# Experts' rows without a token are skipped in the gather and in the store, which becomes an indirect transfer

## The reference, cut to what matters

```python
expert = g_idx * EXPERTS_PER_GROUP + e_idx            # 2 of 32 experts for each of T = 512 tokens
order, counts = argsort(flat_e), bincount(flat_e)     # 1024 (token, expert) pairs
x_rows = hf[row_tok]                                   # rows of each expert's block
y = (silu(xb @ w_e_gate[e]) * (xb @ w_e_up[e])) @ w_e_down[e]      # 1024->512, 1024->512, 512->1024
y = segment_sum(y_rows * row_w, row_tok)               # back to the tokens
out = rmsnorm(x + y)
```

## Time and profile before

| | |
|---|---|
| median of 3 runs | 2750.77 us |
| the profiled execution's own time | 2743.79 us |
| its span, first to last instruction | 2742.1 us |
| mean granted TensorE clock | 0.979 of full speed |
| experts, first store of a result to last | 2192.81 to 2710.28 us |
| busy over the whole span | PE 94%, DVE 72%, ACT 46%, POOL 37% |
| instructions | 38302 |

### The profile page before, as it was taken

One profiled execution on the slowest core, in us unless ns is written; L12 is line 12 of the kernel. 1 busy time (PEld: TensorE's weight loads), 2 busy tenths in 40 slices (PEclk: granted clock), 3 DMA queues, 4 the chain that ended last, 5 costly groups with the idle time before them and its releaser, 6 DMA issues. The chain is left out here.

```text
span 2742.1 us, 38302 instructions
## 1 busy us (share of the span) xinstructions
PE 2588.0 (94%) x13813; PEld 1281.3 (47%) x13813; DVE 1962.7 (72%) x3255; ACT 1252.2 (46%) x1316; POOL 1008.0 (37%) x724
## 2 busy tenths in 40 slices
PE   8989999999999999999999899999999699998994
PEld 4465444444444544444444454555544344444441
DVE  5545887988855635888888754466543699999996
ACT  5434323323234432333333343444432589888884
POOL 0000000177776746888888200000001355334331
PEclk9989999999999999999999999999999799999997
DMA  5301874344446478999999532221113599999995
GB/s 215 108 16 55 287 280 182 120 161 147 170 146 153 163 182 284 364 366 362 366 365 365 216 125 94 91 75 65 62 67 141 224 393 393 392 393 402 398 389 191
DMA packets 175580, 614.83 MB, mean 224 GB/s; under 512 B 58336, under 2 KB 74720, under 8 KB 125792
## 3 DMA queue, kind: packets, MB, share of 16 engines
q1 hardware_dynamic: 57312, 411.62, 39.6%
q0 software_dynamic: 47712, 127.12, 12.8%
q10 hardware_dynamic: 70432, 74.46, 8.9%
HBM read 539.59 MB, written 73.53 MB: 224 GB/s over the span
## 5 line engine op out<-in xcount | busy, mean ns | idle before, releaser
L738 PE MATMUL ps<-a_hi,w_hi 128*128 128x512 bf16 (+3 forms) x1768 | 648.3, 369 | 8.0 <-ACT xn L1499 2.9
L740 PE MATMUL ps<-a_hi,w_lo 128*128 128x512 bf16 (+3 forms) x1768 | 648.6, 369 | 0.0
L739 PE MATMUL ps<-a_lo,w_hi 128*128 128x512 bf16 (+3 forms) x1768 | 648.6, 369 | 0.0
L738 PE MATMUL ps<-w_hi,arena 128*128 128x512 bf16 (+1 forms) x1344 | 514.0, 382 | 11.9 <-DVE arena L2176 9.9
L739 PE MATMUL ps<-w_lo,arena 128*128 128x512 bf16 (+1 forms) x1344 | 512.3, 381 | 0.0
L740 PE MATMUL ps<-w_hi,arena 128*128 128x512 bf16 (+1 forms) x1344 | 512.2, 381 | 0.0
L2026 DVE TENSOR_TENSOR w_lo<-w_st,w_hi 128x2048 bf16<-128x2048 f32 x127 | 290.5, 2290 | 221.8 <-ACT w_hi L1493 122.6
L1493 ACT ACTIVATE w_hi<-w_st 128x2048 bf16<-128x2048 f32 x127 | 242.4, 1909 | 337.9 <-PE ps L740 305.1
L624 POOL DMA_INDIRECT gate_dram<-arena x256 | 321.2, 1255 | 85.4 <-issue 79.3
L1499 ACT ACTIVATE xn<-ps 128x512 f32<-128x512 f32 x128 | 76.2, 597 | 440.9 <-PE ps L740 334.7
L738 PEld LDWEIGHTS ps<-a_hi,w_hi 128*128 128x128 bf16 x1768 | 173.4, 98 | 194.1 <-issue 9.7
(11 more groups left out here) (410 smaller groups left out, 4069.9 us busy)
## 6 DMA issues: line engine op xcount, KB each, us to landing
w_st<-in_w_all SPq DMA_DIRECT2D x260, 1024.0 KB
arena<-in_w_all SPq DMA_DIRECT2D x64, 1024.0 KB
act_dram<-xn POOLq DMA_DIRECT2D x64, 512.0 KB
xn<-in_w_all SPq DMA_DIRECT2D x32, 1024.0 KB
arena<-act_dram ACTq DMA_DIRECT2D x64, 384.0 KB
gate_dram<-xn ACTq DMA_DIRECT2D x14, 1536.0 KB, 8.4
arena<-gate_dram ACTq DMA_DIRECT2D x64, 336.0 KB
a_hi<-in_w_all SPq DMA_DIRECT2D x16, 1024.0 KB
```

The costliest lines, as they stand in the source:

```text
L738: pe.matmul(dst, l_hi, r_hi, start=start, stop=False)
L739: pe.matmul(dst, l_hi, r_lo, start=False, stop=False)
L740: return pe.matmul(dst, l_lo, r_hi, start=False, stop=stop)
```

## The change

Two row lists get values outside their range for slots without a token, and the indirect DMAs get a bounds check that lets such rows be left out. The store of results becomes an indirect DMA with its own list of destination rows. `y_dram` is filled with finite numbers early on, and `x_g` is set to zero once.

```diff
+NO_ROW = 4096
+NO_CELL = 1 << 20
...
+            pool.wait_ge(gla_y, TB)
+            finite = w_all[0:NE * CAP * D // (P * CW)].rearrange("n p x -> (n p x)")
+            half = NE * CAP * D // 2
             for r in range(2):
-                pool.dma_start(first_st[:, r, :], cols_in[:, 0:4]).then_inc(y_stored[r], 16)
+                pool.dma_start(y_dram.rearrange("q r d -> (q r d)")[r * half:(r + 1) * half].rearrange("(n x) -> n x", x=D),
+                               finite[r * half:(r + 1) * half].rearrange("(n x) -> n x", x=D)).then_inc(y_stored[r], 16)
...
+            pool.memset(x_g[0:CAP, :, :, :].rearrange("p b a d -> p (b a d)"), 0.0)
+            pool.drain()
             pool.wait_ge(x_st, 16 * TB)
...
                 pool.indirect_dma_start(x_g[0:CAP, p, :, :].rearrange("p a d -> p (a d)"), None, x_dram,
-                                        bass.IndirectOffsetOnAxis(ap=rows[0:CAP, p:p + 1], axis=0)).then_inc(xe_ld[p], 16)
+                                        bass.IndirectOffsetOnAxis(ap=rows[0:CAP, p:p + 1], axis=0),
+                                        bounds_check=T - 1, oob_is_err=False).then_inc(xe_ld[p], 16)
...
             def store(r, i, c):
+                at = y_idx[0:CAP, c % 2:c % 2 + 1]
                 pool.wait_ge(y_out, moe(r, i, c) + 2)
-                pool.dma_start(y_dram[moe(r, i, c)], y_st[0:CAP, c % 2, :]).then_inc(y_stored[c % 2], 16)
+                pool.tensor_tensor(at, y_at[0:CAP, bass.ds(2 * i + c, 1)], zero_i[0:CAP, 0:1], ALU.add)
+                pool.drain()
+                pool.indirect_dma_start(y_dram.rearrange("q r d -> (q r) d"), bass.IndirectOffsetOnAxis(ap=at, axis=0),
+                                        y_st[0:CAP, c % 2, :], None, bounds_check=PASSES * NE * CAP - 1, oob_is_err=False).then_inc(y_stored[c % 2], 16)
+                pool.drain()
...
-                    dve.scalar_tensor_tensor(tok_now[:, s, :], blk_f[:, 0, s, :], now, tok_f[:, :], ALU.is_equal, ALU.mult)
+                    dve.scalar_tensor_tensor(tok_now[:, s, :], blk_f[:, 0, s, :], now, tok_1[:, :], ALU.is_equal, ALU.mult)
...
+            dve.tensor_scalar(tok_1, tok_f[:, :], 1.0, None, ALU.add)
+            dve.tensor_scalar(y_base[0:CAP, :], iota_f[0:CAP, 0:NE], float(CAP), tok_f[0:CAP, 0:1], ALU.mult, ALU.add)
...
                 dve.wait_ge(rt_sum, r + 1)
-                dve.tensor_copy(row_i[0:CAP, 0:NE], ps[0:CAP, 5, 0:NE]).then_inc(rt_row, 1)
+                dve.tensor_scalar(row_n[0:CAP, :], ps[0:CAP, 5, 0:NE], 0.0, float(NO_ROW), ALU.is_equal, ALU.mult)
+                dve.drain()
+                dve.scalar_tensor_tensor(row_i[0:CAP, 0:NE], ps[0:CAP, 5, 0:NE], -1.0, row_n[0:CAP, :], ALU.add, ALU.add)
+                dve.scalar_tensor_tensor(y_at[0:CAP, :], row_n[0:CAP, :], float(NO_CELL // NO_ROW), y_base[0:CAP, :], ALU.mult, ALU.add)
+                dve.drain().then_inc(rt_row, 1)
```

More of the change, by code:

```diff
@@ L362, in build_program @@
         row_i = view(o, NE + 1, dt=I32); o += NE + 1
+        row_n = view(o, NE); o += NE
+        tok_1 = view(o, TB); o += TB
+        y_base = view(o, NE); o += NE
+        y_at = view(o, NE, dt=I32); o += NE
+        y_idx = view(o, 2, dt=I32); o += 2
         idx = view(o, 2, dt=I32); o += 2
@@ L2472, in first @@
                     rows_of_pass(r)
+                    dve.tensor_scalar(y_base[0:CAP, :], y_base[0:CAP, :], float(NE * CAP), None, ALU.add)
                 dve.wait_ge(rt_sum, r + 1)
-                dve.tensor_copy(row_i[0:CAP, 0:NE], ps[0:CAP, 5, 0:NE]).then_inc(rt_row, 1)
+                dve.tensor_scalar(row_n[0:CAP, :], ps[0:CAP, 5, 0:NE], 0.0, float(NO_ROW), ALU.is_equal, ALU.mult)
[3 more added lines that the diff above has]
+                dve.drain().then_inc(rt_row, 1)
                 if not isinstance(r, int):
```

## The result

| | before | after |
|---|---|---|
| median | 2751.73 us (4 runs beside the kernel after) | 2861.12 us (4 runs, 2858.33 to 2867.19) |
| ratio after / before | | 1.0401, 95% interval 1.0378 to 1.0424 |
| span of the profiled execution | 2742.1 us | 2861.9 us |
| mean granted TensorE clock | 0.979 | 0.955 |

The account below looks back on a forecast made before the run. Compute, then DMA, bounds the loop before; after, POOL's serial store and gather. 8.4 + 13.2 - 2.8 gives 18.8 us per expert, span 2265.4 + 28 x 18.8 = 2791.8, timed 2800 us; range 2729 to 2900.

Parts of the forecast that it names:

- POOL nearly full, a drain lasting to the landing, its series becomes the loop's pace: Experts' loop: drains already hold POOL 14.9 of 16.1 us; store and gather in series then set the pace.
- DVE in POOL's way: Experts' loop: DVE contends with POOL for SBUF, costing up to 1.7 us per copy and 4.7 per gather issue.
- The rows' bytes, 17 to 19 us alone: Experts' loop: half the gathered and stored rows left out, 8.4 MB less DMA, alone worth 17 to 19 us.
- S: POOL's store per expert, from register operations to drained landing: 7.7 to 15.4 us with all rows, taken as 8.4.
- G: POOL's gather behind the store, from copy to drained landing: 8.6 to 15.3 us, taken as 13.2 before relief.
- The relief of 1.4 us per landing: Store and gather landings: 1.1 us less each from halved rows, 0.3 less each from lighter-loaded DMA engines.
- P as S + G: POOL's period per expert in the loop, store then gather in series: 21.6 less 2.8, so 18.8 us.
- From the span to the time: Whole kernel: the span's increase of 50 us carried over to the median of the runs, giving 2800 us.
- Rival A: Experts' loop: POOL's chain fits and the saved bytes count, 16.1 to 16.5 us per expert, 2733 to 2735; chance 0.27.
- Rival B: Experts' loop: left-out rows shorten no landing, period 21 us, span 2853, or 24 and 2937; chance 0.22.
- The early copy at 0: Two DRAM-to-DRAM DMAs of 8.4 MB behind 265 us: taken as costing 0, bounds 0 and 22 us.
- What would show it: Loop signs: stores some 19 us apart, PE waiting for `x_dram` rows, no ACT weight waits, DMA and DVE near 0.85.

Follow-up runs that it names:

- light DVE: The kernel after, drains kept, with DVE computing its remainder w_lo for only 512 of 2048 columns: 2723.42 us in a single run.
- gather-only kernel: The kernel after with only the gather leaving rows out, the direct store of before and no early DRAM-to-DRAM copy: 2726.3 us, ratio 0.9921 to the kernel before.

## Why the prediction was right in its mechanism and short in size

- *POOL nearly full, a drain lasting to the landing, its series becomes the loop's pace:* right. Without the one drain the loss is gone (0.9925), and the chain runs through both drains.
- *DVE in POOL's way:* right. The Trainium skill, GPSIMD Engine Reference, section Key points, names the contention but no size; the trace agrees, with copies from 0.18 up to 5.00 us and indirect stores from 0.93 to 4.93, and with a light DVE their means are 0.26 and 0.98.
- *The rows' bytes, 17 to 19 us alone:* right, a little low: some 20 by the gather-only kernel, 24 between the two kernels without the store's drain. In the kernel after they are hardly felt, since POOL is the bound.
- *S, the mis-sized term:* this is the step that failed. I took 8.4, less relief 7.0, arguing that the store meets little of DVE because PE has just stood still. Over the 28 rounds S is 9.8, and 28 x 2.8 = 77 us of span come from it: the copy is 1.8 on average for my 0.2, the issue 2.9 for my 0.9. The trace shows the opposite of my argument on the path: the store that counts is released by DVE's add, when DVE is at full pace again, and takes 16.7 us (copy 4.87, gap 0.85 for my 0.3, issue 4.92 and 5.8 to the landing). The store that meets an idle DVE lies in the shadow of the restart.
- *G:* 11.8 taken. Its mean is 10.7, so as a mean it was 1.1 too high, which hides 31 us of the miss. On the path it is 17.4, in the slow expert: I used means of a mixture, and the long form is the one on the path.
- *The relief of 1.4 us per landing:* hardly there where it counts. In the cycle shown the slow store lands 10.7 - 4.92 = 5.8 us after its issue, the slow gather 12.8 - 5.63 = 7.2; over the twelve slow experts the means are 5.6 and 6.7, and before they were 5.8 and 7.0. While PE stands, SP refills the ring and the DMA share is 0.98. The mean over all rounds did fall, to 4.0 and 4.8, but by the fast landings (1.7 and 2.0 in the cycle shown), which come while the DMA engines have little to do (a share of 0.34 from 2391 to 2401 us) and are not on the path.
- *P as S + G:* the cycle is a slow S, a slow G and a restart of 10.1 us for two experts, 22.1 each, where I had 18.8; with the cycles of three it is 21.0 over the loop, 0.6 of it POOL's wait for results, which I had at nothing. I also had PE waiting for every gather. The last one was a fast one and lay ready 9.3 us before PE took its rows at 2791.0. The miss of 70 us of span is 77 for S, -31 for G, 28 x 0.6 or 16 for the waits, and these 9, to within a us.
- *From the span to the time:* the profiled execution of before was 7 us shorter than the median of its runs, so the miss is 61 us by the medians (2861 for 2800).
- *Rival A* needed P below 17.0. It is what happens once the store's drain is gone. *Rival B* came closest by its number (P = 21, span 2853), and its landing without relief is nearly what the slow experts show. Its reason is not seen: with the gather's rows left out the stream of weights gained some 20 us, where loaded halves would have kept it back. And its sum kept my S of 8.4, so that it fits is partly luck.
- *The early copy at 0:* nearly. ACT waits once for a chunk there, 14.2 us, and the first store of activations starts at 363.81 us instead of 361.1, so 2.7 us were on the path of this execution; timed, it can't be told from nothing. *The memset* took 3.54 us, hidden.
- *What would show it:* PE's waits for `x_dram` rows and the end of the waits for weights came as said. So did the share of 0.84, by luck: 16.5 us of transfers in 21.0 would be 0.79, but a MB of weights took 2.66 us (78.5% of 280 for 82.70 MB) for my 2.53. "Stores some 19 us apart all through" did not come, and DVE is at 0.75, not 0.85.

What stays open: why PE stands at every second or third expert (the trace shows the cycles, not what selects them), and how the 49 us between the kernel before with copy and drains and the kernel with all rows and an indirect store divide between the indirect store's issue and its landing.

## What to carry to other kernels

Ask of each drain on the queue that issues DMAs which transfers are in flight there. One that stands between two transfers puts their landings in series, while behind both it is free as long as the sum stays under the loop's period. When a chain comes within a microsecond or two of the period, price it at both ends, not by means alone: in this loop, once POOL was late, it was released by the busy engine's own result and met that engine at full pace, so its long forms were on the path and its short ones in the shadow. For skipped rows, take the bytes where DMA is the bound, and put no drain between the store and the next gather; handing over the index list by a semaphore, one turn ahead, does as well.

## What the runs showed that I had not expected

- A drain on POOL also waits for a transfer that was issued before the instruction it was written for: 6.10 us between a copy and a store, ending with the landing of a gather.
- More work on VectorE made a kernel 19 us faster, and 60 us in a single run with more of it, with POOL's instructions shorter beside it (a gather's issue 0.95 us on average, where it was 2.96).
- A 64-element copy of GpSimd takes 4.87 us (0.18 alone) beside VectorE's instructions back to back: it begins at 2592.60 us, and ends at 2597.47 with the second `w_lo` (2597.43). An indirect issue takes up to 5.64 us in this kernel (0.94 alone), while the direct store's issue took at most 0.59 in the kernels that have it.
- Leaving out half of the rows gave back their bytes' time, but under a full DMA it shortened a gather's landing only from 7.05 to 6.5 us after the issue, and a store's not at all.
